# Modulating after the turn: gain and shift as per-partition columns instead of broadcast rows

## The reference, cut to what matters

```python
def _modulate(x, g, shift, scale):
    return _rmsnorm(x, g) * (1 + scale) + shift
...
m_x = _modulation(c, w_mod[l], b_mod[l])        # 6 rows of 1024: shift, scale, gate, twice
h = _modulate(x, norm1_g[l], m_x[0], m_x[1])
x = x + m_x[2] * mix_x                          # mix_x = _token_mix(h, ...)
h2 = _modulate(x, norm2_g[l], m_x[3], m_x[4])
x = x + m_x[5] * _peer(h2, ...)                 # 128 experts of 16384 for each token
```

## Time and profile before

| | us |
|---|---|
| median of three runs | 4309.7 (4306.75 to 4313.01) |
| the profiled execution: its own time | 4306.61 |
| its span from first to last instruction | 4305.2 |
| PE busy | 3722.5 (86%) |
| DVE busy | 2369.1 (55%) |
| POOL busy | 1300.6 (30%) |
| ACT busy | 601.2 (14%) |
| DMA, mean over the span | 282 GB/s |

### The profile page before, as it was taken

How to read it: one execution, slowest core, us unless ns; L and a number is a source line. 1 busy time by engine, 2 the same in 40 slices (tenths; PEclk the granted TensorE clock), 3 DMA queues, 4 the chain that set the end, 5 groups by cost and what they waited for, 6 DMA issues and landing times. The chain is left out here.

```text
span 4305.2 us, 41073 instructions
## 1 busy us (share of the span) xinstructions
PE 3722.5 (86%) x14696; PEld 2637.1 (61%) x14696; DVE 2369.1 (55%) x5573; ACT 601.2 (14%) x1567; POOL 1300.6 (30%) x1125
## 2 busy tenths in 40 slices
PE   8978899997988679999988998877877999877777
PEld 6667788886847568887846775333334787333333
DVE  3542112367767876766762115777774122877875
ACT  1212100100001110000002101111111221111111
POOL 1100000001664445765640003444441001444442
PEclk9989999998998879999998999998998999899999
DMA  8652334333997769999962338999996235999997
GB/s 322 248 207 97 125 139 184 139 138 125 413 367 283 251 236 363 405 398 366 408 265 90 118 134 355 418 374 382 419 421 256 108 113 227 391 421 421 421 421 317
DMA packets 209546, 1214.93 MB, mean 282 GB/s; under 512 B 23889, under 2 KB 25041, under 8 KB 97729
## 3 DMA queue, kind: packets, MB, share of 16 engines
q0 software_dynamic: 154368, 855.71, 49.7%
q1 hardware_dynamic: 54976, 356.60, 21.9%
HBM read 1211.07 MB, written 1.15 MB: 282 GB/s over the span
## 5 line engine op out<-in xcount | busy, mean ns | idle before, releaser
L1179 PE MATMUL bank<-big 128*128 128x256 f32 (+3 forms) x9848 | 2144.1, 378 | 68.9 <-issue 14.8
L1179 PEld LDWEIGHTS bank<-big 128*128 128x128 f32 x9848 | 1836.8, 192 | 379.0 <-issue 91.8
L2315 POOL DMA_INDIRECT big<-in_pboth,big x1024 | 1230.1, 1201 | 1279.3 <-PE bank L1561 635.4
L1561 PE MATMUL bank<-big 128*128 128x512 f32 x2048 | 1007.6, 651 | 278.4 <-ACT big L2279 278.3
L2013 DVE CUSTOM_DVE_ANT_0 big<-big 128x1024 f32<-128x1024 f32 x768 | 926.9, 1224 | 334.7 <-DMA big<-in_pboth,big 331.0
L1561 PEld LDWEIGHTS bank<-big 128*128 128x128 f32 x2048 | 416.6, 208 | 866.5 <-issue 501.3
L2302 POOL TENSOR_TENSOR big<-big 128x1 f32<-128x1 f32 (+1 forms) x49 | 44.6, 912 | 1565.6 <-DVE big L1615 1565.5
L2024 DVE SCALAR_TENSOR_TENSOR big<-big 128x1024 f32<-128x1024 f32 x254 | 326.2, 1284 | 36.3 <-DMA big<-in_pboth,big 12.9
L2279 ACT ACTIVATE big<-big 128x128 f32<-128x128 f32 x512 | 164.8, 391 | 251.6 <-DVE big L1992 241.5
L1214 PE MATMUL bank<-big 128*128 128x128 f32 x572 | 97.9, 309 | 96.6 <-DVE big L1826 37.7
L1214 PEld LDWEIGHTS bank<-big 128*128 128x128 f32 x572 | 75.7, 161 | 117.2 <-issue 68.3
(11 more groups left out here) (197 smaller groups left out, 2167.4 us busy)
## 6 DMA issues: line engine op xcount, KB each, us to landing
big<-in_w SPq DMA_DIRECT2D x104, 1024.0 KB, 7.3
big<-in_wmod POOLq DMA_DIRECT2D x48, 1024.0 KB, 9.1
big<-in_wgu SPq DMA_DIRECT2D x44, 1024.0 KB, 8.0
big<-in_wzg SPq DMA_DIRECT2D x36, 1024.0 KB, 4.8
big<-in_wro SPq DMA_DIRECT2D x32, 1024.0 KB, 6.8
big<-in_wpq SPq DMA_DIRECT2D x24, 1024.0 KB, 4.8
big<-in_wd SPq DMA_DIRECT2D x22, 1024.0 KB, 8.0
big<-in_pboth,big POOLq DMA_INDIRECT x1024, 12.4
```

The costliest lines, as they stand in the source:

```text
L1179: last = pe.matmul(o, a, b, start=(i == 0), stop=(i == n - 1))
L1561: last = pe.matmul(u.ap, d.ap, row[:, 512 * i:512 * i + 512], start=(k == 0), stop=(k == 127))
L2315: g.indirect_dma_start(out=s.ap, out_offset=None, in_=table, in_offset=bass.IndirectOffsetOnAxis(ap=index, axis=0)).then_inc(s.full[0], 16)
```

## The change

Gain and shift are made once as columns: `modulation` turns each finished part on PE, and DVE copies the turned values into `mcols` and forms the gain columns `gcols` (`mod_columns`, six times). `modulate` no longer loads rows. The two token tiles are only scaled by their reciprocal roots (one on ACT, `row_scale`; one on DVE, `row_scale_v`), turned on PE, and modulated while leaving PSUM: ACT takes the first bank of each tile and DVE the second, four instructions of 128x128 each with a per-partition scale and bias (`col_turn`). For `norm2` the token-major rows are still needed by the experts; they are modulated afterwards (`modulated_rows`: three row loads, `mod_gain`, `mod_row`), in `peer_x` behind the ranking of the first head, in the memory of the last two landing places of the arena. The table load `load_cs` moves ahead of `modulate` and waits for `x` instead of `hT`.

In the diff, `mod_columns` and the two `keep_busy` lines stand in PE's program (`mod_turn` is renamed `col_turn` there), the next two functions in DVE's, the last in ACT's; `places` and `rows` stand in `peer_x`, and `part_end` in `modulation`, called at the fourth weight tile of the following part and at the end.

The columns take 288 more columns of SBUF per partition ahead of the arenas, and `BIG_N` grows by 24. The number of landing places in the arena follows from what is left; the last two of them wait for the rows.

```diff
-        ("qg", 2), ("kvg", 1), ("psc", 2), ("bg", 24)]
+        ("qg", 2), ("kvg", 1), ("psc", 2), ("bg", 24), ("n1", 8), ("n2", 8)]
-BIG_N = 53184
+BIG_N = 53208
+        self.mcols = whole.get(192, (4, 48))
+        self.gcols = whole.get(64, (8, 8))
...
+        def part_end():
+            l, part, args = late.pop()
+            put("mod_store", **args)
+            u = banks.take()
+            self.cols_ok = u.free
...
+            put("mod_columns", src=args["rows"], u=u, ready=args["ready"], dst=c4, gains=gains)
...
     def mix_phase(self, banks, wr, sm, ar, l, X, vec, rope_on):
+        if rope_on:
+            cs = ar.get(512, (2, 256), parts=96)
+            cs_ok = self.tick("d_cs", 16)
+            self.put("load_cs", cs=cs, done=cs_ok, before=[self.x_ok])
...
+    def modulate(self, banks, sm, X, l, vec, which, h, hT):
...
+        for tt in range(1 if r0 else 0, 2):
+            put("row_stats", src=X[:, tt, :], dump=h[:, tt, :], r=rs[tt], ready=ready)
+        yield 3
+        done = [tick("rows_scaled"), tick("rows_scaled_v")]
+        put("row_scale", src=X[:, 0, :], dst=h[:, 0, :], by=sm[:, 8:9], r=rs[0], done=done[0], ready=ready)
+        put("row_scale_v", src=X[:, 1, :], dst=h[:, 1, :], by=sm[:, 9:10], r=rs[1], done=done[1])
+        yield 3
+        for tt in range(2):
+            us = [banks.take() for _ in range(2)]
+            put("col_turn", h=h[:, tt, :], us=us, dst=hT[:, :, tt * P:(tt + 1) * P], ...)
+            yield 3
+        return [u.free for u in us]
...
+        dgs = Ring([Slot(ar.get(128)) for _ in range(5)])
+        places = [ar.get(2048) for _ in range((ar.size - ar.at) // 2048)]
+        rows = self.modulated_rows(l, 0, 3, "norm2", h2, [places[-2][:, 0:1024], places[-2][:, 1024:2048],
+                                   places[-1][:, 0:1024]], [self.x_ok])
+            if i == 1:
+                for _ in range(4):
+                    next(route)
+                rows_ok = yield from rows(hT_ok)
-        while ar.size - ar.at >= 2048:
-            more(ar.get(2048))
+        for ap in places[:-2]:
+            more(ap)
...
+        for ap in places[-2:]:
+            more(ap, rows_ok)
...
+    def mod_columns(src, u, ready, **_):
+        opened(u)
+        pe.wait_ge(*ready)
+        turn(u, [src[:, b * P:b * P + P] for b in range(4)]).then_inc(u.full[0], 1)
-                    keep_busy(u, 12)
+                    keep_busy(u, 8)
                     pe.wait_ge(*r.done)
-                    keep_busy(u, 7)
+                    keep_busy(u, 2)
...
+    def row_scale_v(src, dst, by, r, done):
+        v.wait_ge(*r.done)
+        v.tensor_scalar(dst, src, by, None, ALU.mult).then_inc(done[0], 1)
+    def col_turn(us, dst, gain, shift, cols_ok, **_):
+        u = us[1]
+        v.wait_ge(*cols_ok)
+        v.wait_ge(*u.full)
+        for k in range(4, 8):
+            i = v.tensor_scalar(dst[:, k, :], turned(u, 4)[:, k - 4, :], gain[:, k:k + 1], shift[:, k:k + 1], ALU.mult, ALU.add)
...
+    def col_turn(us, dst, gain, shift, cols_ok, **_):
+        u = us[0]
+        s.wait_ge(*cols_ok)
+        s.wait_ge(*u.full)
+        for k in range(4):
+            i = s.activation(dst[:, k, :], turned(u, 4)[:, k, :], ACT.Identity, bias=shift[:, k:k + 1], scale=gain[:, k:k + 1])
```

More of the change, by code:

```diff
@@ L642, in modulation @@
         tick("d_ctx", 16)
+        put("mod_zero", parts=[s.ap for s in st.slots])
         put("mod_c", c2=c2, c3=c3, loaded=tick("d_c2", 16), tanh=tick("mod_tanh"), done=tick("mod_c_done"))
@@ L670, in modulation @@
                 rows = self.mods[l].rearrange("v a d -> v (a d)")
-                late.append(dict(dst=[rows[:, 2048 * part + 512 * j:2048 * part + 512 * j + 512] for j in range(4)],
-                    src=[s.ap[32 * j:32 * j + 2, :] for j in range(4)], ready=u.free, done=stored[turn]))
-        put("mod_store", **late.pop())
+                late.append((l, part, dict(rows=s.ap, dst=[rows[:, 2048 * part + 512 * j:2048 * part + 512 * j + 512] for j in range(4)],
+                    src=[s.ap[32 * j:32 * j + 2, :] for j in range(4)], ready=u.free, done=stored[turn])))
+        part_end()
         for w in few:
@@ L696, in modulate, with rows @@
         tick(lane, 32)
[L697 to L713, removed]
+        put("mod_load", gb=gb, sc=sc, sh=sh, srcs=srcs, loaded=tick(lane, 16), before=ready)
+        full = (self.sem(lane), self.counts[lane])
+        def rows(turned):
+            put("mod_gain", gb=gb, sc=sc, loaded=full)
+            yield 1.3
+            for tt in range(2):
+                done = tick("mod_rows")
+                put("mod_row", h=h[:, tt, :], gain=sc, sh=sh, ready=turned, done=done)
+                yield 2.5
+            return done
+        return rows
     def low_rank(self, banks, sm, ws, wt, hT, ready, n, tmp, dst, gcols):
@@ L748, in keys_values, with mixer @@
         return [r, ku[3].free, vu[1].free]
-    def mixer(self, banks, wr, sm, ar, l, hT, hT_ok, X, vec, rope_on):
+    def mixer(self, banks, wr, sm, ar, l, hT, hT_ok, X, vec, rope_on, cs):
         put, tick, t = self.put, self.tick, self.t
-        cs = None
         if rope_on:
-            cs = ar.get(512, (2, 256), parts=96)
-            put("load_cs", cs=cs, done=tick("d_cs", 16), before=[hT_ok])
             K, Vv = ar.get(2048, (8, 256), parts=96), ar.get(1024, (2, 512))
@@ L1010, in peer_c @@
         ar, mark, h2, act, gat, eix, gl, hT, hT_ok, keys, rest = got
+        m3 = ar.at
+        rows = self.modulated_rows(l, 1, 3, "norm2", h2, [ar.get(1024) for _ in range(3)], self.b_free)
+        rows_ok = yield from rows(hT_ok)
+        ar.at = m3
         qts = Ring([Slot(ar.get(512, (2, 256)))])
+        qts.slots[0].freed = rows_ok
         tvs = [ar.get(128, (8, 16)) for _ in range(2)]
@@ L1819, in mod_gain, with mod_row, mod_zero, mod_columns @@
         step(v.scalar_tensor_tensor(sc, sc, 1.0, gb, ALU.add, ALU.mult))
-    def mod_row(X, h, by, gain, sh, r, done, **_):
-        v.wait_ge(*r.done)
+    def mod_row(h, gain, sh, ready, done):
+        for ok in ready:
+            v.wait_ge(*ok)
         settled()
-        step(v.scalar_tensor_tensor(h, X, by, gain, ALU.mult, ALU.mult))
+        step(v.tensor_tensor(h, h, gain, ALU.mult))
         settled()
         v.tensor_tensor(h, h, sh, ALU.add).then_inc(done[0], 1)
+        v.wait_ge(*done)
+    def mod_zero(parts):
+        for a in parts:
+            step(v.memset(a, 0.0))
+        settled()
+    def mod_columns(u, dst, gains, **_):
+        v.wait_ge(*u.full)
+        src = turned(u, 4).rearrange("p b (j r) -> p r j b", j=4)[:, 0:2]
+        if gains:
+            step(v.tensor_copy(dst, src))
+            settled()
+            for i, (gain, scale, norm) in enumerate(gains):
+                o = v.scalar_tensor_tensor(gain, scale, 1.0, norm, ALU.add, ALU.mult)
+                if i:
+                    o.then_inc(u.free[0], 1)
+                else:
+                    step(o)
+        else:
+            v.tensor_copy(dst, src).then_inc(u.free[0], 1)
+        v.wait_ge(*u.free)
+    def row_scale_v(src, dst, by, r, done):
[4 more added lines that the diff above has]
+        v.wait_ge(*cols_ok)
+        v.wait_ge(*u.full)
+        for k in range(4, 8):
+            i = v.tensor_scalar(dst[:, k, :], turned(u, 4)[:, k - 4, :], gain[:, k:k + 1], shift[:, k:k + 1], ALU.mult, ALU.add)
+        i.then_inc(u.free[0], 1)
     def low_rank(n, dst, gcols, r, parts, **_):
```

62 lines of the change are left out of this document (36 added, 26 removed).

## The result

The changed kernel takes 4333.9 us (median of five, 4330.85 to 4339.56) against 4310.05 for the kernel before beside it: ratio 1.0057, interval 1.0042 to 1.0073. It is slower by 24 us; the forecast was 30 us faster. A second measurement in another job gave 1.0039 (1.0027 to 1.0051). The profiled execution has a span of 4329.6 us.

What follows compares the result with a forecast made beforehand. PE bounds the vectors' modulation, gathers the expert loops, single chains the fronts between. Terms -19.0 - 12.1 - 9.5 + 0.6 + 7.9 + 2.6 = -29.5 gave 4280.2 us on the median; range 4260 to 4300.

Steps and rivals of the forecast that it cites:

- The two ahead of the experts: Chain from X complete to the experts' first query, both layers: 17.4 us shrinks to 7.9, saving 9.5 each.
- the one of layer 1's mixing: Chain ahead of layer 1's mixing: 20.1 us shrinks to 8.0, saving 12.1, with weights no longer last.
- layer 0's mixing: Front ahead of layer 0's mixing: 8.8 us saved, 16 if `peer_add` falls ahead of DVE's row-load wait; taken as 9.5.
- the bank: Modulation of the vectors: PE waits 3.2 us for DVE's bias addition at two of four places, 6.4 us lost.
- the six turns: Modulation of the vectors: six turns of four blocks on PE, 0.134 us each block, add 3.2 us.
- The gains behind it: End of the vectors' stage: 5 us back from PE's 9.5 us weight wait, 4 of its 4.1 us row wait.
- the keys in layer 0's loop: Context keys in layer 0's expert loop: DVE now waits for the turn, twice, mostly covered by the queue; 4 us lost.
- a rival at 0.20: DVE's waits in the context keys cost their full 16 us, not 4, as gathers stop: 4292 us, chance 0.20.
- The place itself: Expert loops, one landing place less: 2.6 us a layer, plus twice 2.6 for earlier dips in layer 0.
- the rival by which places bind: Expert loops: landing can't fall below 12.9 us, so ten places give 2.90 us a gather: 4391 us, chance 0.06.
- The sign that the prediction had named for its own error: Expert loops: DMA share falling from 0.96, or PE's start waiting for a DMA, would show the prediction wrong there.
- `peer_c`: Modulation call in `peer_c`: covered by PE's products, costed at nothing; uncovered it would be one front of 9.5 us.

Runs made afterwards that it cites:

- b_skip: The kernel before, with the ring of two banks moved on by one after each part of the modulation, nothing turned: ratio 1.0069.
- a_own: The changed kernel, with a part's columns turned into the bank in which that part was summed: ratio 0.9971 to the kernel before.
- a_both: The changed kernel, with columns turned into the part's own bank and the context's keys modulated by ACT alone: ratio 0.9957 to the kernel before.

## Why the prediction was wrong

*The fronts were right, one of them partly by luck.* 12.5, 9.7, 11.0 and 9.7 us against 9.5, 9.5, 12.1 and 9.5. The two ahead of the experts and the one of layer 1's mixing came by the steps that were named: the last releaser is `col_turn`, and no weight ends last. In layer 0's mixing `peer_add` did not go ahead of the wait: it fell between the two turns, where PE waits 8.5 us for DVE. DVE had five context rows to do behind the last scaling of X before, 7.0 us, and one, 1.3 us, after:

```profile
2272.56 1.28 DVE L2110 SCALAR_TENSOR_TENSOR big<-big 128x1024 f32<-128x1024 f32 x1
...
2284.48 1.94 PE L1260 MATMUL bank<-big 128*128 128x128 f32 x8 [8.47 <-DVE big L1904]
```

So 5.7 of the 12.5 us come from the context being further ahead, and not from the shorter chain. Counted from the end of the last row the front got 6.8 us shorter, where 8.8 were forecast.

*The term that failed first: the bank.* The prediction saw that all parts from the third on use one bank, and priced it at 6.4 us: "at two of four places, at the other two other products lie between". That step took the addition to run when PE delivers. DVE is in order too, and at the covered places its own work for the first block, on products that PE had only just done, came first: 8.0 us each, not 0, and at the other two 3.1. The waits are 22.2 us, the six turns at 0.66 some 4 (forecast 3.2), and 3.9 us fall away that PE had waited for a weight in this stage before. By difference some 9 of the 31.6 are the slower products behind the waits, for which the prediction had no term. b_skip, without turns, has 26.8 of it. The gains behind it came as said: PE's wait for the weight fell by 5.9 (forecast 5), that for the rows by its 4.

*The term that failed second: the keys in layer 0's loop.* Taken at 4, "the queue covers most", with 16 as a rival at 0.20. DVE's waits are 16.0 us together, and the queue covered little: 13 to 14 us by the traces of the loop, while the ratios of three pairs say 11 or 19, 6 and 7, each with some 7 to 10 either way. The rival was nearer than the term. The place itself cost 13.4 us against the 10.4 of the terms, and the rival by which places bind fell: landing went to 10.6 us, below the 11.4 named as its limit. The sign that the prediction had named for its own error showed: the DMA share fell to 0.94 in layer 0's loop and to 0.56 in the stretch of the keys.

*What the prediction did not have: SP's order in the first block.* `peer_c` was costed at nothing because PE's products cover it. They do, but its loads wait in SP's queue ahead of the first block's weights, and where before PE had products in hand for all but 1.35 us of that wait, it now has none: 7.96 us, 6.6 more. That the new yields moved this point is likely, but no run shows it by itself. Why the first block lost some 7 us more isn't settled.

*The mixing of layer 0,* 6.6 us longer, has the same products. The stretch of it that lost, after, and the same work 24 us earlier in before, columns as in the earlier trace rows:

```profile
2365.00:2415.00 50.00, 43.26 (x200) 36.95 (x201) 9.08 (x27) 15.99 (x39) 0.00 (x0) 0.76 0.07 23
```

```profile
2341.00:2391.00 50.00, 40.34 (x235) 33.53 (x235) 10.61 (x30) 16.89 (x41) 0.00 (x0) 0.97 0.18 65
```

The granted clock is 0.76 in the one and 0.97 in the other. The stage takes 281 to 284 us in the four traces of the kernel before and its versions, and 290 to 291 in eight of the twelve of the changed kernel and its versions. In the other four it takes 284 to 286, a_own among them, whose instructions up to there have the same order as those of a_both, which has 291. So the longer stage was seen only with the change, but not in all its executions; its cause stays open.

## What to carry to other kernels

A resource taken once more from a ring shifts everyone's turn in it: count who gets which buffer afterwards, and for each new wait look at what stands ahead of the releasing instruction on its own engine, not only at what the waiting engine could do meanwhile. A step moved into a busy loop must not make the engine that frees the buffers wait for the engine that is behind. And a buffer that costs nothing in steady flow is the reserve for the stalls: price it at the worst stall, not at the mean pace.

## What was not expected of the hardware

Waits of PE of 3 and 8 us are paid twice here: the products behind them run at the 1.2 GHz level (16 of a part in 3.60 us at a granted clock of 0.50, elsewhere 1.90), and the granted clock of the whole stretch from 40 to 290 us fell from 0.96 to 0.89. And the same dependencies gave the same waits to 0.01 us in two different programs (3.06, 8.04, 7.97, 3.09), while runs of one program differ by up to 0.4% (the kernel before beside b_skip: 4305.4 to 4322.3 us).
